# Recurrent stage of a hybrid decoder step: z and y with features on partitions, the gate behind the transposition, sums of squares by products with ones

## The chip, the cores and the metric

One core of a Trainium2 chip. The metric is the device time of one execution in microseconds, median of the runs. All tensors of this stage are float32; a float32 matrix product is two instructions on TensorE for each 128-row block of weights.

## The reference

One step of a decoder layer, for a prompt of 1024 rows and 8 sample rows. The change touches the Mamba-2 branch. In it 2048 inner features are 4 groups of 512 (8 heads of 64), and the scan goes over 8 chunks of 128 rows. Per group and chunk:

```
y = y_diag + y_off + d_skip * x                # the chunked scan
y = y * silu(z)                                # z = h @ w_in[:, 0:2048]
yg = y.reshape(B, L, 4, 512)
yg = yg * rsqrt(mean(yg * yg, axis=-1) + 1e-6)
y = yg * norm_g                                # then projected by the next stage
```

The sample rows take one step of the same recurrence with their own states, read from memory and written back.

## The kernel before

The function ssm holds the stage. Each engine runs a program of its own, in the order written; semaphores tie them. PSUM has eight banks of 128 x 512.

For each of 4 groups there is a z part, then a scan.

**z part.** TensorE makes z with rows on partitions: 16 units (z_unit), each 8 products of 256 columns into bank 1 or 2, which ScalarE's Silu takes to SBUF (L1740). After every 8 units z_samples makes the sample rows' z with features on partitions, 32 instructions of 8 columns (L1602, two z_samples a group). In between stand the turn of the last chunk before, raw_rows (L1611, L1617), and two spreads (L1628) of the sample rows' B and C, after which VectorE updates half of the sample states (L1851 to L1868). The states' buffer is exchanged by DMA between the halves; in groups 1 and 2 the sync queue does this behind a weight load that waits until half of z is done. The part ends with the samples' sum of squares (L1656).

**Scan.** For chunk c TensorE's order is: front(c + 1), the x/B/C units of the next group but the last one (unit, L1514, 8 products of 344 columns each; 3, 3, 2, 2, 2, 2, 2, 2 units in the chunks), back(c), turn(c - 1), and the last unit. Group 3 has no units. front is: B turned and C·B (L1532, L1533) into bank 0; x turned (L1538) into bank 3; segment sums (L1544). back is: y_diag (L1557), y_off (L1564), state product (L1572). turn transposes y of a chunk into bank 0 (L1581).

VectorE: in front, mask and B copy from bank 0 (L1892, L1893), xdt (L1898), mask product (L1903); in back, y additions (L1914 to L1922), gate by z (L1925), state scaled and added (L1935, L1937), then the mean (L1940); in scale, reciprocal and product by it (L1946, L1947); then, in some chunks, the convolution of a finished x/B/C block (L1803 to L1807), which waits until ScalarE has kept its last unit.

ScalarE: copy of x (L1701) and Exp (L1705) of the next chunk, Silu of a convolved block, copies of units (keep, L1694), out: four copies scaled by norm_g from bank 0 (L1725), then norm: Square with its sum by row (L1713) and Sqrt of one column (L1716).

GpSimd: xw, xd (L1485, L1487), segments of the next chunk (L1453), and the store of turned y (L1446).

## Time and profile before

| what | us |
|---|---|
| median of 3 runs | 3235.45 (3233.89 to 3241.91) |
| profiled execution, its own time | 3245.16 |
| its span | 3243.4 |
| recurrent stage, first product to last store issued | 1105.8 to 1972.1 |
| TensorE busy in the span | 2934.5 (90%) |
| VectorE busy | 1595.4 (49%) |
| ScalarE busy | 729.8 (23%) |
| GpSimd busy | 715.6 (22%) |

The stage is 27% of the span. Times in the rows below are in us from the span's start, means of groups in ns. A bracket behind a row is the engine's idle time ahead of it and what ended that. In the names PE is TensorE's products, PEld its weight loads, DVE VectorE, ACT ScalarE, POOL GpSimd. A row of a timeline merges equal instructions that follow each other; its length goes to the end of the last, which still runs when the next instruction starts.

### The profile page before, as it was taken

Reading aid. Unit: us, or ns where it says so; the run is one execution under the profiler, and the core shown is the slowest. Engines: PE = TensorE matmul, PEld = TensorE weight load, DVE = VectorE, ACT = ScalarE, POOL = GpSimd, SP = SyncE. Lnnn points to the kernel's source line nnn. Section 1 sums busy time; section 2 is a strip of 40 time slices with the busy share of each in tenths; the row PEclk is TensorE's granted clock in tenths of the full one; section 3 lists DMA queues with packets and bytes.
Section 4 is the critical chain, followed back from the end, with each engine's and each line's share of the span. In section 5 each row is a group of like instructions: output and inputs, shape, how many; then the busy total and the mean of one; then the engine's idle time right before and its main releaser. Section 6 shows DMA issues by size and latency. Waiting matters only on the chain. (4 is left out here: it accounts for less than half of the span.)

```text
span 3243.4 us, 39578 instructions
## 1 busy us (share of the span) xinstructions
PE 2934.5 (90%) x15831; PEld 2380.4 (73%) x15831; DVE 1595.4 (49%) x2860; ACT 729.8 (23%) x1511; POOL 715.6 (22%) x430
## 2 busy tenths in 40 slices
PE   6999999989986679999999974999879999999997
PEld 3888566657874556676775854999869898898986
DVE  1313499625541456536546464254563544445355
ACT  4121211126761114424324242000030000000001
POOL 0000520023200122222122232323232232232320
PEclk7999999989995779999999977999989999999999
DMA  6110245410012230121120105233211111111111
GB/s 194 37 66 20 66 137 162 129 49 2 2 39 73 94 86 23 47 78 39 48 75 29 40 26 186 78 112 98 88 31 60 39 39 53 39 46 46 40 40 53
DMA packets 220308, 211.59 MB, mean 65 GB/s; under 512 B 15257, under 2 KB 201489, under 8 KB 219938
## 3 DMA queue, kind: packets, MB, share of 16 engines
q1 hardware_dynamic: 195580, 162.36, 16.5%
q10 hardware_dynamic: 20944, 34.86, 3.1%
q0 software_dynamic: 3600, 11.82, 0.9%
q8 instruction: 127, 2.08, 0.3%
q14 instruction: 57, 0.47, 0.0%
HBM read 165.32 MB, written 43.83 MB: 64 GB/s over the span
## 5 line engine op out<-in xcount | busy, mean ns | idle before, releaser
L2052 PE MATMUL ps<-h_lo,w_hi 128*128 128x344 f32 x1504 | 483.0, 321 | 40.3 <-DVE h_lo L2160 33.5
L2054 PE MATMUL ps<-h_hi,w_lo 128*128 128x344 f32 x1504 | 481.5, 320 | 0.0
L2053 PE MATMUL ps<-h_hi,w_hi 128*128 128x344 f32 x1504 | 481.5, 320 | 0.0
L2052 PEld LDWEIGHTS ps<-h_lo,w_hi 128*128 128x128 f32 x1504 | 284.2, 189 | 42.0 <-issue 35.4
L2053 PEld LDWEIGHTS ps<-h_hi,w_hi 128*128 128x128 f32 x1504 | 283.9, 189 | 0.2
L2054 PEld LDWEIGHTS ps<-h_hi,w_lo 128*128 128x128 f32 x1504 | 284.0, 189 | 0.0
L2034 POOL CAST w_hi<-w_raw 128x2048 fp32r<-128x2048 f32 (+1 forms) x50 | 97.3, 1945 | 838.1 <-PE ps L2054 803.4
L1514 PE MATMUL ps<-hT,ring 128*128 128x344 f32 x864 | 266.7, 465 | 0.0
L1593 PE MATMUL ps<-ring,hT 128*128 128x256 f32 x1024 | 236.3, 393 | 7.8 <-PEq L1164 6.7
L453 PE MATMUL ps<-ring,hT 128*128 128x256 f32 (+3 forms) x1152 | 238.1, 369 | 1.0 <-PEq L214 1.0
L1514 PEld LDWEIGHTS ps<-hT,ring 128*128 128x128 f32 x864 | 168.2, 197 | 92.6 <-issue 19.1
L2036 POOL TENSOR_TENSOR w_lo<-w_raw,w_hi 128x2048 fp32r<-128x2048 f32 (+1 forms) x50 | 233.7, 4673 | 4.0
L1593 PEld LDWEIGHTS ps<-ring,hT 128*128 128x128 f32 x1024 | 201.4, 198 | 42.0 <-issue 11.0
L604 PE MATMUL ps<-hT,ring 128*128 128x344 f32 x768 | 229.6, 459 | 0.0
L453 PEld LDWEIGHTS ps<-ring,hT 128*128 128x128 f32 (+1 forms) x1152 | 197.4, 182 | 39.1 <-issue 3.8
L604 PEld LDWEIGHTS ps<-hT,ring 128*128 128x128 f32 x768 | 145.7, 192 | 82.5 <-issue 5.4
L2440 ACT ACTIVATE f_silu<-ps 128x344 f32<-128x344 f32 x66 | 30.3, 459 | 734.6 <-PE ps L2054 734.6
L2473 DVE TENSOR_TENSOR f_prod<-ps,f_silu 128x344 f32<-128x344 f32 x66 | 34.1, 516 | 326.0 <-ACT f_silu L2440 326.0
L667 DVE TENSOR_SCALAR_CACHE_REDUCE reached<-score,threshold_bits 128x384 uint8<-128x384 f32 (+5 forms) x192 | 171.5, 943 | 38.8 <-POOL score L560 36.6
L2052 PE MATMUL ps<-w_lo,a_hi 128*128 128x512 f32 (+1 forms) x396 | 158.1, 399 | 21.4 <-DVE f_scaled L2486 21.4
L874 DVE CUSTOM_DVE_ANT_0 prob<-ps,sel_bias 128x128 f32<-128x128 f32 (+7 forms) x128 | 96.8, 756 | 153.0 <-PE ps L805 151.6
L2053 PE MATMUL ps<-w_hi,a_hi 128*128 128x512 f32 (+1 forms) x396 | 156.4, 395 | 0.0
(393 smaller groups left out, 5025.5 us busy)
## 6 DMA issues: line engine op xcount, KB each, us to landing
ring<-in_w_ada SPq DMA_DIRECT2D x24, 1024.0 KB, 7.5
ring<-in_w_in SPq DMA_DIRECT2D x23, 1024.0 KB, 5.2
w_raw<-in_w_ffn_in SPq DMA_DIRECT2D x44, 512.0 KB, 5.2
ring<-in_w_in SPq DMA_DIRECT2D x24, 512.0 KB, 8.3
w_raw<-in_w_ffn_out SPq DMA_DIRECT2D x10, 1024.0 KB, 5.0
s_sig<-sig ACTq DMA_DIRECT2D x16, 516.0 KB, 6.9
x<-s_sig ACTq DMA_DIRECT2D x16, 516.0 KB, 3.4
stt<-in_state_ssm SPq DMA_DIRECT2D x32, 256.0 KB, 3.9
```

Source lines behind the costliest of these rows:

```text
L453: mm = nc.tensor.matmul(ps[0:r, (9 * s + t) % 4, 0:width], hT[:, k, P * t:P * t + r], w[:, k, 0:width], start=(k == 0), stop=(k == KB - 1))
L604: mm = nc.tensor.matmul(ps[:, j % 4, 0:CW], w[:, k, 0:P], hT[:, k, CW * c:CW * c + CW], start=(k == 0), stop=(k == KB - 1))
L667: a = v.tensor_scalar(reached[:, at:at + P * (i + 1)], score_of(i), thr_f[:, i:i + 1], None, ALU.is_ge, ALU.add, accum_out=count[:, i:i + 1])
L874: nc.vector.tensor_tensor_reduce(out=prob[:, n % 2, 0:L], in0=ps[:, 2 * (n % 2):2 * (n % 2) + 2, :].rearrange("p a n -> p (a n)")[:, chunk ...
L1514: a = mm(ps[:, 6 + u % 2, 0:CW], w[:, k, P * (f % 2):P * (f % 2) + P], hT[:, k, CW * c:CW * c + CW], start=(k == 0), stop=(k == KB - 1))
L1593: a = mm(ps[:, 1 + u % 2, 0:256], hT[:, k, P * t:P * t + P], w[:, k, :], start=(k == 0), stop=(k == KB - 1))
L2034: self.nc.gpsimd.tensor_copy(hi, raw).then_inc(self.hi_done, 1)
L2036: self.nc.gpsimd.tensor_tensor(lo, raw, hi.bitcast(F32), ALU.subtract).then_inc(self.split, 1)
L2052: nc.tensor.matmul(out, ah, bl, start=(i == 0), stop=False)
L2053: nc.tensor.matmul(out, ah, bh, start=False, stop=False)
L2054: mm = nc.tensor.matmul(out, al, bh, start=False, stop=(i == len(terms) - 1))
L2473: v.tensor_tensor(prod[:, i % 2, :], ps[:, 2 * (i % 3) + 1, 0:CW], silu[:, i % 2, :], ALU.mult).then_inc(act_done, 1)
```

## The change

z is made with features on partitions: 12 units a group (4 feature blocks x 3 column parts of 344, which contain the sample rows), so z_samples goes. y is no longer gated and normalized before it is turned: turn takes it as soon as it is summed. VectorE then multiplies the turned y in PSUM by z (gate). ScalarE squares it; GpSimd adds the halves of the squares (fold); TensorE sums them over partitions with two products by a tile of ones into bank 0 (sum_squares), which also spreads the sum over all partitions. ScalarE takes the root from PSUM with scale 1/512 and bias 1e-6 (root). VectorE takes its reciprocal, 128 x 128, and multiplies (divide); ScalarE scales by norm_g in place (out). In front the product for bank 0 moves behind the segment sums and waits for a root instead of an output. The order of each engine's steps changes with it; in chunk c: gate and square of c - 1, division and output of c - 2. In the z part raw rows and spreads move to units 8 and 10 in group 0, and to 1, 3 and 9 in the others. In SyncE's queue the weight loads behind z wait for 6 and 12 units instead of the two sample products. Cut to its core:

```diff
+    def fold(g, c):
+        n = TT * g + c
+        pool.wait_ge(ysquared, n + 1)
+        v.tensor_tensor(ysq2[:, 0:2 * P], ysq2[:, 0:2 * P], ysq2[:, 2 * P:4 * P], ALU.add).then_inc(yfolded, 1)
...
             if c + 1 < TT:
                 segments(g, c + 1)
             if c >= 2:
-                store(g, c - 2)
+                fold(g, c - 2)
+            if c >= 3:
+                store(g, c - 3)
+        fold(g, TT - 2)
+        store(g, TT - 3)
+        fold(g, TT - 1)
         store(g, TT - 2)
         store(g, TT - 1)
...
-        if n:
-            pe.wait_ge(cb_done, 2 * n)
         if g and c == 0:
-            pe.wait_ge(yT_done, n)
             pe.wait_ge(s_done, n)
         if c >= 2:
-            pe.wait_ge(yT_done, n - 2)
             pe.wait_ge(s_done, n - 1)
-        tr(ps[:, 0, P:2 * P], post[:, 4, cols], K.ident[:])
-        mm(ps[:, 0, 0:P], post[:, 4, cols], post[:, 5, cols], start=True, stop=True).then_inc(bcb_ps, 1)
...
+        if n:
+            pe.wait_ge(cb_done, 2 * n)
+        if g and c == 0:
+            pe.wait_ge(yroot2, n)
+        if c >= 3:
+            pe.wait_ge(yroot2, n - 2)
+        tr(ps[:, 0, P:2 * P], post[:, 4, cols], K.ident[:])
+        mm(ps[:, 0, 0:P], post[:, 4, cols], post[:, 5, cols], start=True, stop=True).then_inc(bcb_ps, 1)
...
     def turn(g, c):
         n = TT * g + c
-        pe.wait_ge(ynormed, n + 1)
+        pe.wait_ge(*((y_ready, n - g) if c else (yd_done, 2 * (n + 1))))
         pe.wait_ge(cb_done, 2 * min(n + 3, TT * (g + 1)))
-        if c == TT - 1:
-            pe.wait_ge(yT_done, n)
+        if c >= TT - 2:
+            pe.wait_ge(yroot2, n)
         for j in range(4):
             t = tr(ps[:, 0, P * j:P * j + P], y[:, c % 2, P * j:P * j + P], K.ident[:])
         t.then_inc(yT_ps, 1)

+    def sum_squares(g, c):
+        pe.wait_ge(yfolded, TT * g + c + 1)
+        for j in range(2):
+            a = mm(ps[:, 0, 0:P], K.ones[:], ysq2[:, P * j:P * j + P], start=(j == 0), stop=(j == 1))
+        a.then_inc(ysum_ps, 1)
...
-        i, t, w = u // TT, u % TT, slab_of(K, slab(g, 3 + u // TT))
-        if t == 0:
-            pe.wait_ge(*ring_landed(K, slab(g, 3 + i)))
...
-            pe.wait_ge(z_done, 2 * TT * g + u - 1)
...
-            a = mm(ps[:, 1 + u % 2, 0:256], hT[:, k, P * t:P * t + P], w[:, k, :], start=(k == 0), stop=(k == KB - 1))
+            a = mm(ps[:, 1 + u % 2, 0:CW], w[:, k, P * (f % 2):P * (f % 2) + P],
+                   hT[:, k, CW * c:CW * c + CW], start=(k == 0), stop=(k == KB - 1))
         a.then_inc(z_ps, 1)
-
-    def z_samples(g, i):
-        w = slab_of(K, slab(g, 3 + i))
-        if g:
...
-        for fb in range(2):
-            for k in range(KB):
-                a = mm(ps[:, 4, DEC * (2 * i + fb):DEC * (2 * i + fb) + DEC], w[:, k, P * fb:P * fb + P],
-                       hT[:, k, SEQ:NT], start=(k == 0), stop=(k == KB - 1))
-        a.then_inc(zs_ps, 1)
...
-        raw_at, spread_at = (1, 4) if g else (10, 13)
-        for u in range(2 * TT):
+        raw_at, spread_at = (1, 3) if g else (8, 10)
+        for u in range(ZU):
             z_unit(g, u)
-            if u == 0 and g:
+            if g and u == 0:
                 turn(g - 1, TT - 1)
                 final_state(g - 1)
+            if g and u == 1:
+                sum_squares(g - 1, TT - 1)
             if u == raw_at:
                 raw_rows(g)
             if u == spread_at:
                 spread(g, 0)
-            if g and u == 12:
+            if g and u == 9:
                 spread(g, 1)
-            if u % TT == TT - 1:
-                z_samples(g, u // TT)
         if g == 0:
             spread(g, 1)
...
+            if c:
+                sum_squares(g, c - 1)
     turn(GROUPS - 1, TT - 1)
+    sum_squares(GROUPS - 1, TT - 1)
...
-    def norm(g, c):
+    act.wait_ge(eps_set, 1)
...
+    def square(g, c):
         n = TT * g + c
         act.wait_ge(ygated, n + 1)
         if n:
-            act.wait_ge(ysquared, n)
-        a.activation(ysq2[:], y[:, c % 2, :], ACT.Square, accum_out=stat[:, 0, c % 2:c % 2 + 1])\
-            .then_inc(ysquared, 1)
-        act.wait_ge(ymean, n + 1)
-        a.activation(stat[:, 2, c % 2:c % 2 + 1], stat[:, 1, c % 2:c % 2 + 1], ACT.Sqrt).then_inc(yroot2, 1)
+            act.wait_ge(ysum_ps, n)
+        a.activation(ysq2[:], yT[:, c % 2].rearrange("p k n -> p (k n)"), ACT.Square).then_inc(ysquared, 1)
+
+    def root(g, c):
+        n = TT * g + c
+        act.wait_ge(ysum_ps, n + 1)
+        if n:
+            act.wait_ge(ynormed, n)
+        a.activation(spreads[:, 0, :], ps[:, 0, 0:P], ACT.Sqrt, bias=eps[:, 0:1], scale=1.0 / GW).then_inc(yroot2, 1)

...
-        act.wait_ge(yT_ps, n + 1)
-        if n >= 2:
-            act.wait_ge(yT_out[c % 2], 16 * (n // 2))
+        act.wait_ge(ynormed, n + 1)
         for j in range(4):
             k = 136 + 4 * g + j
-            o = a.activation(yT[:, c % 2, j, :], ps[:, 0, P * j:P * j + P], ACT.Copy, scale=K.vecs[:, k:k + 1])
+            o = a.activation(yT[:, c % 2, j, :], yT[:, c % 2, j, :], ACT.Copy, scale=K.vecs[:, k:k + 1])
...
-        for u in range(2 * TT):
-            i, t = u // TT, u % TT
-            act.wait_ge(z_ps, 2 * TT * g + u + 1)
+        for u in range(ZU):
+            f, c = u // TC, u % TC
             if g and u == 0:
-                act.wait_ge(ygated, TT * g)
-            a.activation(z[:, t, 256 * i:256 * i + 256], ps[:, 1 + u % 2, 0:256], ACT.Silu).then_inc(z_done, 1)
+                out(g - 1, TT - 2)
+                square(g - 1, TT - 1)
+            act.wait_ge(z_ps, ZU * g + u + 1)
+            a.activation(zT[:, f, CW * c:CW * c + CW], ps[:, 1 + u % 2, 0:CW], ACT.Silu).then_inc(z_done, 1)
             if u == 0 and g:
+                keep_final(g - 1)
+            if u == 1 and g:
+                root(g - 1, TT - 1)
                 out(g - 1, TT - 1)
-                keep_final(g - 1)
...
+            if c >= 2:
+                out(g, c - 2)
             if c:
-                out(g, c - 1)
+                square(g, c - 1)
             for j in units[-1:]:
                 keep(g + 1, j)
-            norm(g, c)
+            if c:
+                root(g, c - 1)
...
+    out(GROUPS - 1, TT - 2)
+    square(GROUPS - 1, TT - 1)
+    root(GROUPS - 1, TT - 1)
...
-                link(v.tensor_tensor(yc, yc, t, ALU.add), ystep, ny)
-            else:
-                dve.wait_ge(yd_done, 2 * (n + 1))
-            v.tensor_tensor(yc, yc, z[:, c, :], ALU.mult).then_inc(ygated, 1)
+                v.tensor_tensor(yc, yc, t, ALU.add).then_inc(y_ready, 1)
...
-            i = c % 2
-            dve.wait_ge(ysquared, n + 1)
-            v.tensor_scalar(stat[:, 1, i:i + 1], stat[:, 0, i:i + 1], 1.0 / GW, EPS, ALU.mult, ALU.add).then_inc(ymean, 1)
...
-        def scale(c):
+
+        def gate(c):
             n = TT * g + c
-            i = c % 2
+            dve.wait_ge(yT_ps, n + 1)
+            if n >= 2:
+                dve.wait_ge(yT_out[c % 2], 16 * (n // 2))
+            v.tensor_tensor(yT[:, c % 2], ps[:, 0, :].rearrange("p (k n) -> p k n", k=4), zT[:, :, P * c:P * c + P],
+                            ALU.mult).then_inc(ygated, 1)
+
+        def divide(c):
+            n = TT * g + c
             dve.wait_ge(yroot2, n + 1)
-            link(v.reciprocal(stat[:, 3, i:i + 1], stat[:, 2, i:i + 1]), ystep, ny)
-            v.tensor_scalar(y[:, i, :], y[:, i, :], stat[:, 3, i:i + 1], None, ALU.mult).then_inc(ynormed, 1)
+            v.reciprocal(spreads[:, 0, :], spreads[:, 0, :]).then_inc(yinv, 1)
+            dve.wait_ge(yinv, n + 1)
+            v.tensor_tensor(yT[:, c % 2], yT[:, c % 2], spreads[:, 0, :].unsqueeze(1).to_broadcast([P, 4, P]),
+                            ALU.mult).then_inc(ynormed, 1)
...
         front(0)
         for c in range(TT):
             if c + 1 < TT:
                 front(c + 1)
             back(c)
-            scale(c)
+            if c >= 2:
+                divide(c - 2)
+            if c:
+                gate(c - 1)
             if g + 1 < GROUPS:
                 for f in blocks_at[c]:
                     convolve(g + 1, f)
+        divide(TT - 2)
+        gate(TT - 1)
+        divide(TT - 1)

```

## Rows read from the trace of the kernel before

**Rows 1.** Stretches: length, busy PE, PEld, DVE, ACT, POOL, granted clock, DMA.
```profile
1105.81:1165.02 59.21, 59.21 (x269) 51.62 (x269) 30.17 (x42) 12.99 (x23) 6.14 (x7) 0.90 0.27 87
1247.75:1352.69 104.94, 97.02 (x392) 63.94 (x391) 68.81 (x94) 47.59 (x83) 23.73 (x20) 0.95 0.11 36
1473.35:1579.83 106.48, 98.55 (x393) 64.73 (x392) 68.83 (x94) 47.57 (x83) 23.75 (x20) 0.94 0.10 35
1698.72:1802.35 103.63, 95.70 (x392) 63.30 (x391) 68.82 (x94) 47.57 (x83) 23.75 (x20) 0.97 0.10 36
1352.69:1428.00 75.31, 73.65 (x357) 63.24 (x356) 29.22 (x50) 14.84 (x34) 15.50 (x15) 0.94 0.25 72
1579.83:1653.48 73.65, 71.99 (x358) 61.81 (x356) 29.22 (x50) 14.84 (x34) 15.50 (x15) 0.96 0.25 74
1802.35:1876.31 73.96, 72.30 (x357) 62.15 (x356) 29.22 (x50) 14.84 (x34) 15.50 (x15) 0.95 0.18 51
1902.94:1950.64 47.70, 35.38 (x140) 23.22 (x141) 30.54 (x52) 24.98 (x45) 18.78 (x16) 0.79 0.05 21
```

**Rows 2.** TensorE's timeline in group 3's z part (start, length, line, operation).
```profile
1824.21 10.52 PE L1593 MATMUL ps<-ring,hT 128*128 128x256 f32 x48
1834.57 3.63 PE L1602 MATMUL ps<-hT,ring 128*128 128x8 f32 x32
1838.06 19.20 PE L1593 MATMUL ps<-ring,hT 128*128 128x256 f32 x80
1857.09 1.88 PE L1628 MATMUL ps<-bc_diag,ones 128*128 128x512 f32 x4
...
1873.91 1.88 PE L1656 MATMUL ps<-ysq,ones 128*128 128x8 f32 x8 [0.81 <-DVE ysq L1874]
```

**Rows 3.** VectorE's timeline, end of the sample work in that part.
```profile
1869.61 0.19 DVE L1871 TENSOR_TENSOR ysum<-ysum,xdt_s 128x32 f32<-128x32 f32 x1
```

**Rows 4.** TensorE's timeline in the scan of group 2.
```profile
1718.97 0.27 PE L1532 MATMUL ps<-ident,post 128*128 128x128 f32 x1
...
1727.82 1.08 PE L1564 MATMUL ps<-state,post 128*128 128x512 f32 x2
...
1730.03 4.79 PE L1514 MATMUL ps<-hT,ring 128*128 128x344 f32 x16
1734.66 0.27 PE L1532 MATMUL ps<-ident,post 128*128 128x128 f32 x1
...
1747.22 1.10 PE L1572 MATMUL ps<-xw,btok 128*128 128x512 f32 x2 [2.64 <-DVE xdt L1898]
...
1753.22 0.27 PE L1532 MATMUL ps<-ident,post 128*128 128x128 f32 x1
...
1765.79 1.31 PE L1572 MATMUL ps<-xw,btok 128*128 128x512 f32 x2 [2.64 <-DVE xdt L1898]
...
1773.47 0.27 PE L1532 MATMUL ps<-ident,post 128*128 128x128 f32 x1
```

**Rows 5.** VectorE's timeline there: the state addition of the first chunk.
```profile
1731.71 0.69 DVE L1937 TENSOR_TENSOR state<-state,ps 128x512 f32<-128x512 f32 x1
```

**Rows 6.** VectorE's groups of instructions (xcount | busy us, mean ns): reciprocals.
```profile
L1946 DVE RECIPROCAL ssm_stat<-ssm_stat 128x1 f32<-128x1 f32 x32 | 5.2, 164 | 39.8 <-ACT ssm_stat L1716 39.8
...
L1279 DVE RECIPROCAL dt_t<-dt_t 128x264 f32<-128x264 f32 x1 | 1.8, 1802 | 0.0
```

**Rows 7.** GpSimd's groups of instructions: an addition of two SBUF tiles.
```profile
L559 POOL TENSOR_TENSOR score<-score,score_term 128x384 f32<-128x384 f32 x3 | 3.0, 992 | 0.2
```

**Rows 8.** ScalarE's timeline in the scan of group 2.
```profile
1681.68 1.28 ACT L1705 ACT_TABLE_LOAD   x1
1682.98 1.02 ACT L1705 ACTIVATE m<-ps 128x1024 f32<-128x1024 f32 x1
...
1719.52 0.63 ACT L1713 ACTIVATE ssm_ysq<-ssm_y 128x512 f32<-128x512 f32 x1
...
1730.23 1.14 ACT L1725 ACTIVATE ssm_yT<-ps,vecs 128x128 f32<-128x128 f32 x4 [3.50 <-PE ps L1581]
```

More of the change, by code:

```diff
@@ L1320, in ssm @@
         posts = sb("post", [P, 2, FBS, SEQ])
-        z = sb("z", [P, TT, GW])
+        zT = sb("zT", [P, 4, NT])
         tail = sb("tail", [P, FBS, 11])
@@ L1326, in ssm @@
         cx, ct = sb("cx", [P, FBS, DEC]), sb("ct", [P, FBS, DEC])
-        zs, xdt_s = sb("zs", [P, 4, DEC]), sb("xdt_s", [P, 4, DEC])
+        xdt_s = sb("xdt_s", [P, 4, DEC])
         bc_diag = sb("bc_diag", [P, 2, 4, P])
@@ L1340, in ssm @@
         yT = sb("ssm_yT", [P, 2, 4, P])
-        stat = sb("ssm_stat", [P, 4, 2])
+        spreads = sb("ssm_rms", [P, 1, P])
+        eps = sb("ssm_eps", [P, 1])
         fin = sb("fin", [P, 4, P])
@@ L1359, in ssm @@
         yo_done, s_scaled, s_done, yd_done = K.sem("yoff_done"), K.sem("state_decayed"), K.sem("state_done"), K.sem("ydiag_done")
-        ystep, ygated, ysquared, ymean, yroot2, ynormed = (K.sem(n) for n in (
-            "y_step", "y_gated", "y_squared", "y_mean", "y_root", "y_normed"))
+        y_ready, ygated, ysquared, yfolded, ysum_ps, yroot2, yinv, ynormed = (K.sem(n) for n in (
+            "y_ready", "y_gated", "y_squared", "y_squares_folded", "y_squares_summed", "y_root", "y_inverse", "y_normed"))
         yT_ps, yT_done, yT_out = K.sem("ssm_yT_in_psum"), K.sem("ssm_yT_done"), [K.store_sem(f"ssm_yT_stored{i}") for i in range(2)]
@@ L1364, in ssm @@
         old_out = K.store_sem("old_conv_rows_stored")
+        eps_set = K.sem("eps_set")
         block = ctx.enter_context(nc.Block())
+        ZU = 4 * TC
         here = [3, 3, 2, 2, 2, 2, 2, 2]
@@ L1442, in _ @@
             v = nc.gpsimd
+            v.memset(eps[:], EPS).then_inc(eps_set, 1)
             v.memset(pre[:, :, 0:CONV - 1], 0.0).then_inc(conv_step, 1)
@@ L1783, in _ @@
             v = nc.vector
-            nconv, nss, ny = [0], [0], [0]
+            nconv, nss = [0], [0]
             def link(ins, sem, count):
```

23 lines of the change are left out of this document (12 added, 11 removed).

## The prediction

> **What bounds the kernel now.** I read the page's totals first, to see which engine is nearly full: TensorE is, so its idle time is what can be won, and what is added to it is paid. Then the busy time by stretch, cut at the edges of the recurrent stage's parts [rows 1]. The stage runs from about 1105.8 to 1972 us. In each of the four groups a z part (sums for z, and the sample rows' states beside them) is followed by a scan of eight chunks. In the scans of groups 0 to 2 the x/B/C sums of the next group fill TensorE (97.02 of 104.94 us busy). In the scan of group 3 nothing fills it: 35.4 of 47.7 us busy in four chunks, granted clock 0.79 [rows 1]. There a loop of waits sets the time, 47.70 / 4 = 11.93 us a chunk. The timelines of the engines then show what sets each part.
>
> In a z part TensorE has 16 units of 3.45 us (three of them from 1824.21 to 1834.57) and twice 32 products of 8 columns for the sample rows, 3.49 us each time (1834.57 to 1838.06) [rows 2]. The 5 units behind the first of these took 19.03 us (1838.06 to 1857.09) instead of 17.25. VectorE's sample work ends 12.7 us after the second spread (1857.09 to 1869.80) [rows 2, 3]: there is slack before 1873.91 now, but not much.
>
> In the scan of group 2 a chunk without other waits takes 15.69 us (1718.97 to 1734.66); where a convolution ran before, the state product waits 2.64 us for xdt. Behind one such wait TensorE needed 7.68 us for state product, turn and unit (1765.79 to 1773.47), behind another 6.00 (1747.22 to 1753.22): its clock had fallen to the lower level in the first and not in the second [rows 4].
>
> **The change part by part.**
>
> *z in 12 units of 344 columns.* The removed 256-column units and the new ones have the same work: 16 x 3.45 = 55.2 us against 12 x 4.63 = 55.6 us, 4.63 us being what a unit of this shape takes now (1730.03 to 1734.66) [rows 4]. The sample products go: 2 x 3.49 us. Groups 1 to 3, counted from the end of the last x/B/C unit: up to the second spread there are now 13 units, one set of sample products, 1.8 us of slower clock (19.03 against 17.25), and 4.6 us of other things (1857.09 - 1802.35 = 54.7). After it: 10 units (46.3), the same 4.6, two new sums of squares at 0.44 each: 51.8. Then VectorE's sample work, which no longer hides behind 3 units and samples (13.9 us) but only behind 2 units (9.3 us): 12.7 us and two small operations, 0.5 with their gaps, until the sum may start, 13.2. With the 2.40 us up to the scan's first product (1873.91 to 1876.31) that makes 67.4 us against 75.31, 73.65 and 73.96 [rows 1, 2, 3]: -7.9, -6.3, -6.6. The second half of the states reaches VectorE barely in time: its exchange now starts after 6 units, and I estimate that it is complete about 1 us before it is needed.
> Group 0: the raw rows come after 9 units, not 11, and the first spread after 11 units, not 14. The 59.21 us up to it are 14 units (48.3), one set of sample products (3.5) and 7.4 of raw rows and slow clock [rows 1]. Of the 7.4 I let half go with the sample products, behind which the clock was slow, as in rows 2, and keep 3.9 for raw rows and the start: 11 x 4.63 + 3.9 = 54.8. What follows waits for the states' transfer, which that spread sets off. So only 4.4 us of the larger saving counts.
> z parts: **-25 us**.
>
> *The y chain.* VectorE loses the wait for Square and for Sqrt. It loses 0.69 (gate), 0.49, 0.16 and 0.15 us of work, and gets a gate from PSUM (0.69), a reciprocal of 128x128 and a product of 128x512 (0.69). No row shows that reciprocal. With one column it took 164 ns, with 264 columns 1802 ns: (1802 - 164) / 263 = 6.2 ns a column, so 0.95 us [rows 6]. The bounds are 0.16 and 1.80; the slope decides for 0.95. The fold on GpSimd (two inputs in SBUF, 256 columns) lies below the 0.992 us of 384 columns and above two thirds of it, 0.66: I take 0.72 [rows 7]. The root on 128 columns from PSUM I take as 0.37, above a quarter of the 1.14 us that four such operations took together, which overlap [rows 8]; it lies on the chain only at the end. The sum of squares is four passes of 128 columns, 0.44 us (as four transposes), 0.85 at the low clock.
>
> All of this hangs in one chain in program order, and TensorE, also in order, stands at its end. Sum of squares c-1 comes ahead of everything of the next chunk. It needs: VectorE's state addition of chunk c, division c-2, gate c-1; ScalarE's output scaling c-2, then Square c-1; GpSimd's fold. In groups 0 to 2 one x/B/C unit is to cover that.
> Let Y be the start of the y_off product (1727.82). VectorE started the state addition at Y + 3.89 (1731.71); without the gate ahead, 0.72 less, Y + 3.17. Reciprocal at Y + 3.78, product at 4.77, done 5.46. Output scaling holds ScalarE 1.0 us before Square may start: 6.49, done 7.12 (0.63) [rows 4, 5, 8]. Fold done 7.91, sum of squares at Y + 7.95. TensorE by itself is there at Y + 6.84 (1734.66). So it stands 1.1 us in each chunk. From the sum's start to Y it has 8.85 (1718.97 to 1727.82) + 0.44 = 9.29. Period: 9.29 + 7.95 = 17.24 us.
> The convolution is no longer late: it starts as soon as the last unit is kept, and no longer behind Square, mean, Sqrt, reciprocal and scaling, so the three waits of 2.64 us and the slow units behind them go. Chunks 2 to 6 of a group take 5 x 17.24 = 86.2, chunk 7 without a front 0.44 + 4.63 + 1.73 + 7.95 = 14.75: 101.0 against 104.94, 106.48 and 103.63 [rows 1, 4]. That is -12 us in three groups; chunk 0 and 1 stay (chunk 1 has two units ahead and no division yet). For slower clock after the new stops I put 15 x 0.4 = 6 us back, between 0 and 1.7 each (below). Scans 0 to 2: **-6 us**.
>
> *Group 3's scan.* Now the loop closes with the state addition: TensorE's next front starts when it is done. After, it closes with the sum of squares. Behind the state addition's start that is 4.78 us (7.95 - 3.17) where it was 0.72, so +4.06; the sum itself at the low clock +0.85; the gate out of the chain -0.72. The product for B/C moved behind the segment sums takes 0.6 out of the path to Exp, but mask, B copy and xdt now come after it and delay the mask product by 0.7; that product no longer meets GpSimd's segments and takes about 0.7 less. Sum: +3.6, 15.5 us a chunk. It is paid four times between front 3 and front 7 (+14). The start gains 1. The last two chunks pay more, since nothing is left to overlap: front 7's chunk +4, chunk 7 +5, then behind the last state addition. There, where scaling, turn and store took 5 us, stand division, output scaling, Square, fold, sum, root, division, gate, Square, fold, sum, root, division, output scaling and two stores, some 15.5 us at the prices above: +10; less 3 us that turn and division overlap: +16 for the end. Group 3's scan: **+29 us**.
>
> What only moves is hidden: the table load for the root lies beside fold and sum (1.28 against 0.72 + 0.6) [rows 8], and two more in the z part beside 4.6 us units. Stores start later, but land before their buffer is written.
>
> Sum: -25 - 6 + 29 = -2 us. The profiled execution took 3245.16 us, its span 3243.40; the median of the runs is 3235.45, 0.3% less. The difference carries over: 3235.45 - 2 = 3233.
>
> A page's price against this, in sentences of its own. Every switch of ScalarE's table took 1.28 us here, and Exp started with no gap behind it (1681.68, 1682.98) [rows 8]. The Trainium skill (ScalarE: Activation LUTs, "What ACT_TABLE_LOAD costs") adds 1.38 us of drain to each switch, 2.66 in all. By that the root would end 1.3 us later and delay the copy of x behind it; group 3's loop would be about 0.5 us longer, and my -2 would be +2. The trace decides for 1.28.
>
> **The rivals.**
>
> *The clock falls at each new stop (slower).* Of the nine stops of 2.64 us in groups 0 to 2, seven were followed by the lower level, and then 1.7 us were lost (7.68 against 6.00) [rows 4]. If the 1.1 us stops do this as well, 15 x 1.7 = 26 instead of 6: +18, 3253. It decides (over +0.3%) from about 1.2 us a stop. Against it: the stop is shorter, and dense units stand right ahead. Beside this: the Trainium skill (TensorE: Matmul & The Clock Gate, "HAM oscillation") tells of a kernel whose array was throttled again in every iteration by a wait. The trace shows this after 2.64 us, and not after every one.
>
> *The chain is shorter than I price it (faster).* If reciprocal or fold cost what their narrow rows show, or the output scaling from SBUF goes faster, 0.75 us or more leaves the chain. Then TensorE hardly stands: 15 x 0.75 = 11, the clock's 6, and 7 x 0.75 = 5 in group 3 go: -22, 3211; half of it 3222.
>
> *The states' transfer becomes the bound of the z parts.* In groups 1 and 2 I estimate 1 us of slack; if it comes 3 us late and group 0 gains nothing, z gives -15: +8, 3243. That the change gives no saving here at all is excluded by the 28 us of sample products gone, which nothing covers in groups 1 to 3.
>
> **How the numbers follow.** Forecast 0.45, its own range 3222 to 3246; clock 0.20; shorter chain 0.25; states 0.10. Within 0.3% (9.7 us) is what a measurement of this kernel can't tell from no change. Of the forecast 0.06 lies on the faster side of that and 0.04 on the slower; of the clock 0.17 are slower; of the shorter chain 0.20 faster; of the states 0.04 slower. Faster 0.26, same 0.49, slower 0.25. The range takes in most of the clock's case and half of the shorter chain's: 3214 to 3254.
>
> **What would show it.** Right: sum-of-squares products with about 1.1 us of TensorE idle ahead, released by GpSimd's fold, in chunks 2 to 6; no wait for xdt; group 3's chunks near 15.5 us; reciprocals of 0.95 us; z parts of 67 us with 2 us idle ahead of the samples' sum. Wrong: a reciprocal far off 0.95, a scan of group 3 that keeps its present length, or a mean clock under 0.94 in the scans of groups 0 to 2.

## The result, and the profile after

| | forecast | measured |
|---|---|---|
| median, changed kernel | 3233 (3214 to 3254) | 3246.05 us (3241.13 to 3249.25, 15 runs) |
| median, kernel before, beside it | 3235.45 | 3238.44 us (3233.89 to 3247.67, 15 runs) |
| ratio | 0.999 | 1.0018, 95% interval 1.0009 to 1.0026 |

The changed kernel is slower: its median lies 7.6 us (0.23%) higher, and the ratio of all its runs to those of the kernel before is 0.18% over 1. That is less than the 0.3% which the prediction called "same", and 3246 lies in its range, but the interval excludes both "no change" and the small gain that was forecast.

The busy time of the changed kernel by stretch (start, end and length; then busy us of PE, PEld, DVE, ACT, POOL with instructions in brackets; granted clock, DMA share, GB/s): chunks 2 to 7 of groups 0, 1, 2, three z parts, and the scan of group 3.

```profile
1242.93:1346.84 103.91, 95.80 (x417) 63.60 (x415) 71.49 (x90) 49.91 (x79) 31.61 (x26) 1.00 0.10 34
1456.89:1560.80 103.91, 95.80 (x417) 63.60 (x415) 71.48 (x90) 49.89 (x79) 31.59 (x26) 1.00 0.10 34
1672.68:1776.60 103.92, 95.80 (x417) 63.62 (x415) 71.50 (x90) 49.90 (x79) 31.60 (x26) 1.00 0.10 34
1346.84:1412.62 65.78, 63.28 (x236) 41.63 (x237) 31.87 (x50) 17.63 (x34) 17.89 (x18) 1.00 0.31 92
1560.80:1626.86 66.06, 63.55 (x237) 41.90 (x237) 31.87 (x50) 17.64 (x34) 17.89 (x18) 0.99 0.31 93
1776.60:1842.38 65.78, 63.28 (x237) 41.63 (x237) 31.85 (x50) 17.64 (x34) 17.90 (x18) 1.00 0.22 65
1842.38:1970.70 128.32, 75.96 (x314) 50.78 (x314) 64.52 (x96) 46.18 (x78) 42.68 (x40) 0.76 0.04 15
```

Against [rows 1]: the three stretches of six chunks, which took 103.6 to 106.5 us at a clock of 0.94 to 0.97, now take 103.9 each at 1.00. The z parts fell from 75.31, 73.65 and 73.96 to about 65.9. The scan of group 3 went from 95.8 us (1876.31 to 1972.09) to 128.32, and its clock is 0.76. In this pair of traces the whole stage took 866.28 us before and 865.98 after (1104.72 to 1970.70).

The timeline of chunk 2 to 3 of group 2, which answers to [rows 4, 5]:

```profile
1703.28 0.94 DVE L1974 RECIPROCAL ssm_rms<-ssm_rms 128x128 f32<-128x128 f32 x1
...
1704.98 1.28 ACT L1745 ACTIVATE ssm_yT<-ssm_yT,vecs 128x128 f32<-128x128 f32 x4 [6.57 <-DVE ssm_yT L1976]
...
1705.54 0.81 DVE L1831 TENSOR_SCALAR post<-pre,vecs 128x1024 f32<-128x1024 f32 x1
1706.17 0.61 ACT L1731 ACTIVATE ssm_ysq<-ssm_yT 128x512 f32<-128x512 f32 x1
...
1706.86 1.39 POOL L1464 TENSOR_TENSOR ssm_ysq<-ssm_ysq 128x256 f32<-128x256 f32 x1 [11.01 <-ACT ssm_ysq L1731]
...
1708.30 0.71 PE L1603 MATMUL ps<-ssm_ysq,ones 128*128 128x128 f32 x4 [1.79 <-POOL ssm_ysq L1464]
...
1725.05 0.72 POOL L1464 TENSOR_TENSOR ssm_ysq<-ssm_ysq 128x256 f32<-128x256 f32 x1 [10.64 <-ACT ssm_ysq L1731]
1725.32 1.28 ACT L1738 ACT_TABLE_LOAD   x1
...
1725.82 0.71 PE L1603 MATMUL ps<-ssm_ysq,ones 128*128 128x128 f32 x4 [1.13 <-POOL ssm_ysq L1464]
...
1726.61 0.37 ACT L1738 ACTIVATE ssm_rms<-ps,ssm_eps 128x128 f32<-128x128 f32 x1
```

The order is the one foreseen: reciprocal, output scaling (four in 1.28 us), Square, fold, and TensorE waiting for it: 1.13 us at 1725.82. Where a convolution starts on VectorE (1705.54) the fold takes 1.39 us instead of 0.72 and the stop is 1.79. The table load ends at 1726.60 and the root starts at 1726.61. Two chunks of group 3, the sums and what they wait for:

```profile
1867.32 1.22 PE L1603 MATMUL ps<-ssm_ysq,ones 128*128 128x128 f32 x4 [5.05 <-POOL ssm_ysq L1464]
...
1881.34 0.61 ACT L1731 ACTIVATE ssm_ysq<-ssm_yT 128x512 f32<-128x512 f32 x1
...
1882.03 0.72 POOL L1464 TENSOR_TENSOR ssm_ysq<-ssm_ysq 128x256 f32<-128x256 f32 x1 [7.82 <-ACT ssm_ysq L1731]
...
1882.80 1.22 PE L1603 MATMUL ps<-ssm_ysq,ones 128*128 128x128 f32 x4 [6.30 <-POOL ssm_ysq L1464]
```

15.48 us from sum to sum, 6.3 of them TensorE's idle time behind the fold.

### The profile page after: what moved, and what is told of

It is laid out like the page before. It is cut to its first block and busy times, and to the rows that moved or that the text cites. A ratio compares the mean times of both kernels' runs of the same rounds, so it can differ in the third digit from the quotient of the medians.

```text
span 3239.2 us, 38780 instructions
## 1 busy us (share of the span) xinstructions
PE 2897.3 (89%) x15447; PEld 2298.8 (71%) x15447; DVE 1610.9 (50%) x2828; ACT 732.0 (23%) x1457; POOL 754.2 (23%) x463
## 5 line engine op out<-in xcount | busy, mean ns | idle before, releaser
L1528 PE MATMUL ps<-hT,ring 128*128 128x344 f32 x864 | 257.8, 452 | 0.0
L1616 PE MATMUL ps<-hT,ring 128*128 128x344 f32 x768 | 227.9, 457 | 6.8 <-PEq L1164 6.8
L604 PE MATMUL ps<-hT,ring 128*128 128x344 f32 x768 | 227.2, 455 | 0.0
L1528 PEld LDWEIGHTS ps<-hT,ring 128*128 128x128 f32 x864 | 160.7, 190 | 77.6 <-issue 1.4
L1616 PEld LDWEIGHTS ps<-hT,ring 128*128 128x128 f32 x768 | 146.6, 192 | 84.9 <-issue 13.1
L604 PEld LDWEIGHTS ps<-hT,ring 128*128 128x128 f32 x768 | 144.3, 190 | 80.9 <-ACT sig L639 5.4
L2090 PE MATMUL ps<-w_hi,a_lo 128*128 128x512 f32 (+1 forms) x396 | 155.7, 393 | 0.0
```

The source lines that it names most:

```text
L604: mm = nc.tensor.matmul(ps[:, j % 4, 0:CW], w[:, k, 0:P], hT[:, k, CW * c:CW * c + CW], start=(k == 0), stop=(k == KB - 1))
L1528: a = mm(ps[:, 6 + u % 2, 0:CW], w[:, k, P * (f % 2):P * (f % 2) + P], hT[:, k, CW * c:CW * c + CW], start=(k == 0), stop=(k == KB - 1))
L1616: a = mm(ps[:, 1 + u % 2, 0:CW], w[:, k, P * (f % 2):P * (f % 2) + P], hT[:, k, CW * c:CW * c + CW], start=(k == 0), stop=(k == KB - 1))
L2090: mm = nc.tensor.matmul(out, al, bh, start=False, stop=(i == len(terms) - 1))
```

## The experiments

Medians are compared with the changed kernel's 3246.05 us, ratios are to runs of the kernel before on the same chip. The two can disagree by some us: on the four chips of these experiments the kernel before itself had medians of 3241.31 to 3244.68, not 3238.44. "Stage" is taken from a kernel's own trace, from the first z product to the end of the last store of y; it leaves out the final state's store, which makes it 0.7 us shorter than above. In the changed kernel it is 865.1 to 867.6 us, by four traces; it holds nothing of the rest of the program, so it is the safer comparison.

### The z part from both sides

`before_few_samples`: the kernel before with one of the eight products of each sum for the sample rows' z; the sums over the other seven blocks of rows are left out.

```diff
-                    for k in range(KB):
+                    for k in range(1):
                         a = mm(ps[:, 4, DEC * (2 * i + fb):DEC * (2 * i + fb) + DEC], w[:, k, P * fb:P * fb + P],
```

> The kernel before with 2 of the 16 products in each of the eight sets of the sample rows' z (the sum over the other seven blocks of rows is left out). Everything else and all waits stay. Theory of my forecast: a set takes 3.5 us and slows the clock behind it by about 2 us, so 8 sets give about 24 us, and in groups 1 to 3 the samples' own chain behind the second spread gives 3 us of that back once per group: 3.1 + 2 saved ahead of it, 0 to 3 behind. Expected 17 to 22 us faster. Rival (the clock behind the sets has nothing to do with them, and the chain of the sample states already sets the z parts): under 10 us faster.

Measured: 3208.74 us (3205.91 to 3210.65), ratio 0.9895 [0.988, 0.991], stage 826.5 us: 34 us less than the kernel before by the ratio, well over the expectation. Its trace of group 3's z part (TensorE):

```profile
1804.87 0.51 PE L1602 MATMUL ps<-hT,ring 128*128 128x8 f32 x4
1805.23 17.51 PE L1593 MATMUL ps<-ring,hT 128*128 128x256 f32 x80
1822.58 1.88 PE L1628 MATMUL ps<-bc_diag,ones 128*128 128x512 f32 x4
```

A set went from 3.63 to 0.51 us, and the five units behind it from 19.20 [rows 2] to 17.51. That makes some 8 us a group. The steps between the samples' sums of squares became 216.5, 214.2 and 211.7 us, from 225.8, 225.5 and 222.8, so 9 to 11 each. Not all of this is the z part's: from the last x/B/C unit to the samples' sum the three z parts lost 9.1, 7.3 and 8.2 us, but the scans of groups 1 and 2, whose code is the same, lost 4.0 and 2.9 us as well. Of the nine waits for xdt five are followed by slow units in this trace, against seven in that of the kernel before. So about 7 us of the saving lie in the scans. Whether taking out the products brought that about, or this execution showed another of the kernel's own patterns, one trace can't tell; as a price of the sample products alone 34 us is too much.

`after_idle_samples`: the changed kernel with the old sample products put back: 32 of 8 columns each time, into columns of bank 5 that nobody reads.

```diff
+                    if u % 6 == 5:
+                        idle_samples(g, u // 6)
                     z_unit(g, u)
```

> The changed kernel with the kernel before's sample products put back, 32 products of 8 columns ahead of z unit 5 and 32 ahead of unit 11 of each group, into columns of bank 5 that nobody reads (their result is not used). It undoes the saving of the z part alone. Theory: in groups 1 to 3 each set costs its 3.49 us and the slower clock behind it 1.8, less the 2.1 us that TensorE waits for the samples' sum anyway: 4 to 6 us a group, and little in group 0, which waits for the states' transfer: +13 to +20, 3259 to 3266. Rival: what the kernel before lost by these products is what taking out seven eighths of them there gave, 34 us, since each set also costs the clock for long behind it: +30 or more, 3276.

Measured: 3278.40 us (3277.14 to 3282.57), ratio 1.0112 [1.0096, 1.0129], stage 895.7 us: +32 us by the medians and +30.5 by the stage, the rival's size. TensorE in group 3's z part:

```profile
1827.71 3.63 PE L1624 MATMUL ps<-hT,ring 128*128 128x8 f32 x32
1831.20 23.38 PE L1616 MATMUL ps<-hT,ring 128*128 128x344 f32 x80
...
1856.13 4.79 PE L1616 MATMUL ps<-hT,ring 128*128 128x344 f32 x16
1860.76 4.23 PE L1624 MATMUL ps<-hT,ring 128*128 128x8 f32 x32
1864.84 7.64 PE L1616 MATMUL ps<-hT,ring 128*128 128x344 f32 x16
1873.55 1.06 PE L1679 MATMUL ps<-ysq,ones 128*128 128x8 f32 x8 [1.07 <-DVE ysq L1910]
```

The first set costs its 3.49 us alone. The second costs 4.08 (1860.76 to 1864.84), and the unit behind it 7.64 instead of 4.79; only 1.0 of the 2.1 us ahead of the samples' sum hides it. That is 9.4 us a group, and it is measured at 8 to 9 (steps of 225.3, 222.1 and 224.0 us against 216.4, 214.0 and 215.8), and group 0, where I expected little, pays 4.8. So the size was the rival's, without its reason: one unit behind the second set is slow, not many. The z part alone is worth about 30 us, and the scans give it all back.

### The links of the chain

`after_narrow_recip`: the reciprocal works on 1 of its 128 columns; the other 127 stay roots.

```diff
-                    v.reciprocal(spreads[:, 0, :], spreads[:, 0, :]).then_inc(yinv, 1)
+                    v.reciprocal(spreads[:, 0, 0:1], spreads[:, 0, 0:1]).then_inc(yinv, 1)
```

> The changed kernel with VectorE's reciprocal on 1 column in place of 128 (the other 127 columns are multiplied by the root itself: the norm is left out for them). 0.95 us becomes 0.16. Theory (the chain state addition, division, gate, output scaling, Square, fold, sum of squares sets each chunk's end): 0.78 us less in each of the 18 stops of groups 0 to 2, and in 6 to 7 chunks and twice at the end of group 3: 14 + 7 = 21 us faster, and stops of 0.3 to 1.0 us where 1.13 and 1.8 stood. Rival (TensorE's own work sets the chunks and the stops only move): under 5 us faster.

Measured: 3224.87 us (3221.14 to 3233.36), ratio 0.9948 [0.9931, 0.9965], stage 844.4 us: -21 us, as expected. The stop of 1.13 us becomes 0.34 (`after_narrow_recip`, TensorE, group 2):

```profile
1712.37 0.71 PE L1603 MATMUL ps<-ssm_ysq,ones 128*128 128x128 f32 x4 [0.34 <-POOL ssm_ysq L1464]
```

The reciprocal fell from 946 to 156 ns: 0.79 us, all of which left the stop. VectorE is 69% busy in those chunks, yet this operation costs its full length, because the chain passes through it.

`after_no_fold`: TensorE sums four blocks of squares instead of two folded ones.

```diff
-                v.tensor_tensor(ysq2[:, 0:2 * P], ysq2[:, 0:2 * P], ysq2[:, 2 * P:4 * P], ALU.add)
...
-                pe.wait_ge(yfolded, TT * g + c + 1)
-                for j in range(2):
+                pe.wait_ge(ysquared, TT * g + c + 1)
+                for j in range(4):
```

> The changed kernel without GpSimd's fold: TensorE sums the four blocks of squares by four products instead of two of folded ones. Theory: the fold stands in the exposed chain, with 0.72 us, and with 1.39 us where a convolution starts beside it; without it the stop ahead of the sum is 0.38 us everywhere, and two more products cost 0.44 us (0.85 at the low clock). Net 0.3 us in 15 chunks of groups 0 to 2 and 1.0 us in 6, 0.3 us in seven chunks of group 3: 10 to 14 us below the changed kernel, 3232 to 3236, which is below the kernel before. Rival: the convolution is what is late, and the fold beside it only looks long; then the stops of 1.79 us shrink as the others do, by 0.75, and the whole is -6 or less, 3240.

Measured: 3236.67 us (3234.36 to 3237.89), ratio 0.9976 [0.9965, 0.9986], stage 855.7 us: -9 us, just short of the 10 to 14 expected, and below the kernel before. TensorE in group 2, at the sum beside which a convolution starts:

```profile
1703.28 1.16 PE L1599 MATMUL ps<-ssm_ysq,ones 128*128 128x128 f32 x8 [0.33 <-ACT ssm_ysq L1727]
```

All 18 stops of groups 0 to 2 are 0.32 or 0.33 us, those of 1.13 and of 1.79 alike. So the longer fold, and not a late convolution, made the longer stop. In group 3 there is little: stops of 5.0 to 6.2 us in the middle, and four products at the low clock.

### The chain's place

`after_sum_late`: the chain's work is unchanged, but TensorE takes the sum of chunk c - 2, and ScalarE the root of it, behind the next front, in chunks 2 to 7. The last sum but one stays where it was. The sums go to bank 4 (bank 6 in group 3); front waits for the gate instead of the root, and y_off for the root.

```diff
                         front(g, c + 1)
+                    if c > 1:
+                        sum_squares(g, c - 2)
...
-                    if c:
+                    if c and (c == TT - 1):
                         sum_squares(g, c - 1)
```

> The changed kernel with TensorE's sum of squares of chunk c - 1, and ScalarE's root of it, moved one place later, behind the front of chunk c + 2, in chunks 0 to 5 of each group. The sum goes to bank 4 (bank 6 in group 3), so that bank 0 is free after the gate. Theory: TensorE's 1.1 to 1.8 us stop in each chunk of groups 0 to 2 and the 5 to 6.5 us stop in each chunk of group 3 are the price of the chain's place in the program, not of its work. Then the stops of chunks 1 to 6 go (about 4 x 1.13 + 2 x 1.8 = 8 us a group, 24 in three), and group 3's period falls from 15.2 us to about 12 us for five chunks (16 to 20): 40 to 44 us below the changed kernel, near 3203, which would beat both kernels. Rival: the chain only finds another door. The root with its table load now holds ScalarE before the x/B/C copies, and y_off waits for the root: then stops of about 1 us come back at y_off or at the units, and only 10 to 20 us are won, 3226 to 3236.

Measured: 3218.88 us (3216.79 to 3220.11), ratio 0.9927 [0.9914, 0.9941], stage 839.4 us: -27 us, between theory and rival. In groups 0 to 2 the stops ahead of the sums of chunks 1 to 4 are gone; those of chunks 5 and 6 keep theirs, 1.79 and 1.13 us, since chunk 7 has no front to stand behind and the last but one was not moved (two chunks of group 2; TensorE):

```profile
1712.09 1.88 PE L1552 MATMUL ps<-seg,gt 128*128 128x512 f32 x4
...
1714.14 0.61 PE L1611 MATMUL ps<-ssm_ysq,ones 128*128 128x128 f32 x4
1714.59 4.79 PE L1528 MATMUL ps<-hT,ring 128*128 128x344 f32 x16
...
1722.73 1.10 PE L1590 MATMUL ps<-xw,btok 128*128 128x512 f32 x2 [0.71 <-DVE xdt L1938]
```

A wait of 0.71 us for xdt came back in one chunk of each group. In group 3 the period is 13.2 us, not 12: y_off waits 1.33 us for the root, and VectorE's mask product takes 3.70 us beside GpSimd's products, where it took 1.69 in the changed kernel (at 1873.60, beside the last 0.6 us of one). Of these two it is the mask product that counts: the next two experiments have no such wait at y_off in group 3, and their period is 13.2 us as well, with the mask product at 3.69 to 3.71 us (all engines of `after_sum_late`, group 3):

```profile
1865.99 1.04 POOL L1494 TENSOR_TENSOR xw<-xt,s_ddt 128x512 f32<-128x512 f32 x1
...
1866.99 1.04 POOL L1496 TENSOR_TENSOR xd<-xt,heads_row 128x512 f32<-128x512 f32 x1
...
1867.27 3.70 DVE L1943 TENSOR_TENSOR m<-m,cbm 128x1024 f32<-128x1024 f32 x1 [1.59 <-ACT m L1731]
1867.99 1.89 POOL L1457 TENSOR_TENSOR seg<-le,s_dta 128x1024 f32<-128x1024 f32 x1
1868.55 0.37 ACT L1749 ACTIVATE ssm_rms<-ps,ssm_eps 128x128 f32<-128x128 f32 x1
...
1869.06 1.10 PE L1582 MATMUL ps<-state,post 128*128 128x512 f32 x2 [1.33 <-ACT ssm_rms L1749]
```

`after_sum_late_g3`: the same in group 3 alone.

```diff
+                    if c > 1 and g == GROUPS - 1:
+                        sum_squares(g, c - 2)
```

> The same move in group 3 alone; groups 0 to 2 as in the changed kernel. Theory: the +32 us of group 3's scan come from the loop that closes with the fold; with the sum behind the next front five chunks go from about 15.2 to 12 us, 16 to 20 us below the changed kernel (3226 to 3230), which by itself turns the sign against the kernel before. Rival: VectorE's work of a chunk, 8.7 us with the reciprocal, and the turned order set the period as well; then it stays above 14 us and at most 6 us are won (3240).

Measured: 3230.07 us (3228.34 to 3230.89), ratio 0.9959 [0.9945, 0.9972], stage 848.7 us: -16 us. Half of group 3's loss was the sum's place; taking that alone back makes the changed kernel faster than the kernel before. Its period is 13.2 us though y_off waits for nothing (TensorE, group 3):

```profile
1879.29 0.71 PE L1607 MATMUL ps<-ssm_ysq,ones 128*128 128x128 f32 x4 [1.41 <-POOL ssm_ysq L1464]
...
1892.48 0.71 PE L1607 MATMUL ps<-ssm_ysq,ones 128*128 128x128 f32 x4
...
1894.77 1.08 PE L1580 MATMUL ps<-state,post 128*128 128x512 f32 x2
```

`after_sum_later`: the late sum in the last two chunks too. In groups 0 to 2 the sum of chunk 5 stands behind the x/B/C unit of chunk 7. In group 3 all sums go to banks 6 and 7, y_off waits for no root, and at the end the gate of chunk 6 comes ahead of division 5 and its Square ahead of scaling 5.

```diff
                     back(g, c)
+                    if c == TT - 1 and g == GROUPS - 1:
+                        sum_squares(g, c - 2)
...
                     if g and u == 0:
+                        sum_squares(g - 1, TT - 2)
                         turn(g - 1, TT - 1)
```

> The version with the late sum, carried to the last two chunks of each group: the sum of chunk 5 behind the x/B/C unit of chunk 7 (in group 3 behind back of chunk 7), the sum of chunk 6 behind the first z unit of the next group (in group 3 behind the last turn); in group 3 all sums go to banks 6 and 7, so that y_off does not wait for a root, and at its end the gate of chunk 6 and its Square come ahead of the division and scaling of chunk 5. Theory: the stops that are left in that version, 1.79 and 1.13 us in the last two sums of each group, go as well (3 x 2.9 = 9 us), in group 3 the 1.3 us ahead of y_off (up to 6 us) and some 6 us of the two 5.3 us stops at its end: 12 to 20 us below 3218.9, 3199 to 3207. Rival: where nothing fills TensorE, VectorE's mask product, which takes 3.7 us there beside GpSimd's products, sets the period of group 3, and the end is a chain of fixed length: then only the 9 us of groups 0 to 2 come, 3210.

Measured: 3211.78 us (3210.98 to 3215.14), ratio 0.9896 [0.9881, 0.9911], stage 834.4 us: 7 us less than `after_sum_late` by the medians, 5 by the stage, but from the other end than the rival said. From the samples' sum to the last store group 3 takes 106.9 us instead of 117.1. Its period stayed at 13.2 us, in which the rival was right; what fell was the end, which the rival had called a chain of fixed length. Groups 0 to 2 lost 3 us twice (steps of 214.3, 209.8 and 213.4 us against 211.2, 209.8 and 210.7), for a new stop took the place of the old ones (TensorE, start of group 1's z part):

```profile
1347.22 0.61 PE L1613 MATMUL ps<-ssm_ysq,ones 128*128 128x128 f32 x4
1347.66 0.60 PE L1601 MATMUL ps<-ident,ssm_y 128*128 128x128 f32 x4
1351.46 0.63 PE L1660 MATMUL ps<-ident,state 128*128 128x128 f32 x4 [3.19 <-ACT ssm_rms L1757]
1351.92 6.49 PE L1626 MATMUL ps<-hT,ring 128*128 128x344 f32 x16
```

The final state needs bank 4, which holds the sum until its root is taken, and the unit behind the 3.19 us stop is slow.

`after_sum_best`: the final state behind the second z unit.

```diff
                         turn(g - 1, TT - 1)
-                        final_state(g - 1)
                     if g and u == 1:
+                        final_state(g - 1)
                         sum_squares(g - 1, TT - 1)
```

> The version with the late sum in all chunks, with the final state turned behind the second z unit of the next group instead of behind the first, so that its bank's wait for the root of chunk 6 is covered. Theory: the 3.2 us stop ahead of the final state, which ate what the last two sums had given in groups 0 to 2, goes, together with the slow unit behind it: 3 x 3 = 9 us or a little more below 3211.8, 3200 to 3204. Rival: the first two z units then wait for ScalarE, which stands at the root of chunk 6, and the stop only moves to the third unit: 3210.

Measured: 3212.32 us (3206.95 to 3213.10), ratio 0.9904 [0.9888, 0.9921], stage 832.7 us: no change beyond the spread. The rival was right: the same time is lost one step on, ahead of the last sum.

```profile
1350.48 0.60 PE L1660 MATMUL ps<-ident,state 128*128 128x128 f32 x4
1353.48 0.71 PE L1613 MATMUL ps<-ssm_ysq,ones 128*128 128x128 f32 x4 [2.40 <-POOL ssm_ysq L1464]
```

The version without the fold and the four with the late sum beat both kernels; the last two are 1% under the kernel before.

### Several traces of the two kernels

The kernel before was traced seven more times (`before_same`, `before_again`, `before_third`, `before_fourth`, `before_look5` to `before_look7`), the changed kernel three more (`after_same`, `after_third`, `after_fourth`). Their expectations were:

> The kernel before, unchanged, profiled once more. In the first pair of profiles the recurrent stage took 866.3 us before and 866.0 after, yet the medians differ by 7.6 us. Theory A (the sum was made from one execution in which TensorE's clock fell more often than it usually does): here the stage is shorter than 866.3, most likely by 5 to 12 us, all of it in stretches where the granted clock was below 1 the first time (scans of groups 0 to 2, units behind the sample products). Theory B (the two stages are equal, and the 7.6 us arise outside, after or before the stage): the stage takes 866 us within 2 again, and what lies outside it differs.

> The changed kernel, unchanged, profiled once more. The profiled execution was the fastest of 15 (3241.1, median 3246.05). Theory A: this one is nearer the median, and the difference is slow clock: in group 3's scan, or behind the stops of 1.1 to 1.8 us ahead of the sums of squares, which had the full clock the first time. Theory B: the stage takes 866 us within 2 again and the difference to the first profile lies outside it.

> The kernel before once more, for its trace. Theory A: its executions differ by how often the clock falls at the waits for xdt in the recurrent stage; an execution near 3235 would show a stage some 8 us shorter than the 866 us of the two traces so far (3245 and 3247). Theory B: the stage is 866 us in all of them, and what differs lies ahead of it or behind it.

> The kernel before for its trace, a fourth time. The three so far took 3244.5 to 3247.0 us by their own time, all with a stage of 866 us and seven clock falls of nine waits for xdt. Theory A: an execution near 3235 has a shorter stage (fewer falls, 858 us or less). Theory B: the stage is 866 us there too, and it is what lies before and after the stage that is shorter.

> As the one before it: the kernel before once more, theory A a stage of 858 us or less in an execution near 3235, theory B 866 us in every execution.

> The kernel before for its trace. All five traces so far are of executions of 3244.5 to 3249.0 us with a mean granted clock of 0.933 to 0.935, while the timed executions go from 3234 to 3251 us and the fast ones list 0.937 to 0.939. Theory A: the 10 us by which the fast ones are shorter lie in the recurrent stage, as clock falls that do not happen: a trace of an execution under 3240 us shows a stage of 858 us or less and fewer falls behind the waits for xdt. Theory B: they lie outside the stage, where both kernels have the same code: the stage is 866 us in it, and the rest 2367 to 2372 us instead of 2377 to 2382.

> As the look before it. Theory A: in an execution under 3240 us the stage is 858 us or less. Theory B: it is 866 us, and the rest is shorter.

> As the look before it. Theory A: in an execution under 3240 us the stage is 858 us or less. Theory B: it is 866 us, and the rest is shorter.

> The changed kernel for its trace. The kernel before has two stage lengths in eight traces: 865.6 to 866.4 us five times, 861.0 to 861.1 three times, those three in executions of 3239.9 to 3242.5 us; the clock's pattern in the scan of group 3 and in group 2 differs. The changed kernel showed 865.3 and 866.6 us in two traces. Theory A: it has no short pattern to lose or win, since its stops in groups 0 to 2 don't let the clock fall and its group 3 runs at the low level throughout: the stage is 865 to 867 us again. Theory B: it has one too, and the two traces missed it: 861 us or less.

> As the look before it: theory A a stage of 865 to 867 us, theory B 861 us or less in one of the two.

Measured (own time; the stage; the rest of the span, where both kernels have the same code):

| trace | own time | stage | rest |
|---|---|---|---|
| before | 3245.16 | 865.5 | 2377.9 |
| before_same | 3246.98 | 865.8 | 2379.4 |
| before_again | 3244.50 | 866.3 | 2376.4 |
| before_third | 3248.64 | 866.3 | 2380.5 |
| before_fourth | 3248.97 | 866.3 | 2380.9 |
| before_look5 | 3242.45 | 861.0 | 2379.6 |
| before_look6 | 3239.93 | 861.1 | 2377.0 |
| before_look7 | 3240.31 | 861.0 | 2377.5 |
| after | 3241.13 | 865.2 | 2374.0 |
| after_same | 3248.10 | 866.6 | 2379.4 |
| after_third | 3243.59 | 865.1 | 2376.6 |
| after_fourth | 3248.15 | 867.6 | 2378.5 |

The kernel before has two stage lengths, 866 and 861 us; the changed kernel has 865 to 868 only, in four traces. The 861 us lie between what the theories said (858 or 866), so theory A holds in kind and for half the size. The busy time of the middle of group 3's scan shows where most of it is, first of `before_same`, then of `before_look6`:

```profile
1899.00:1947.00 48.00, 35.60 (x144) 23.51 (x144) 30.85 (x53) 24.96 (x44) 19.15 (x17) 0.79 0.05 22
```

```profile
1895.00:1943.00 48.00, 33.72 (x162) 22.69 (x161) 33.27 (x53) 25.98 (x45) 21.34 (x18) 0.89 0.05 22
```

The clock is 0.89 instead of 0.79, and TensorE gets through 162 instead of 144 instructions in the same 48 us. From the samples' sum of group 3 to the last store that is 94.2 us against 97.4 to 97.5. The rest is one clock fall: behind the second wait for xdt of group 1 the state product, turn and unit take 8.8 to 8.9 us in the five traces of 866 and 6.0 in the three of 861 (TensorE, `before_same`, then `before_look6`):

```profile
1523.79 2.04 PE L1572 MATMUL ps<-xw,btok 128*128 128x512 f32 x2 [2.64 <-DVE xdt L1898]
...
1532.63 0.27 PE L1532 MATMUL ps<-ident,post 128*128 128x128 f32 x1
```

```profile
1523.51 1.10 PE L1572 MATMUL ps<-xw,btok 128*128 128x512 f32 x2 [2.64 <-DVE xdt L1898]
...
1529.51 0.27 PE L1532 MATMUL ps<-ident,post 128*128 128x128 f32 x1
```

The traces of 861 us give 1.4 us of this back in the last z part, which takes 72.93 us in `before_look6` and 71.56 in `before_same`. Of the nine waits for xdt seven are followed by slow units in the former, six in the latter.

## Why the prediction was wrong

**The step that failed** is the last line of the sum: "The difference carries over: 3235.45 - 2 = 3233." A gain of 2 us was forecast and the medians show a loss of 7.6. The sum over the stage was nearly right for the pair of traces it was made for: -2 forecast, -0.3 measured (866.28 to 865.98). Part of that is luck, since its three terms were off by -4.2, +2.4 and +3.5 us. But the traced execution lay 9.7 us over the median, and this was subtracted from the changed kernel as well. About 5 us of it were the kernel before's own: its traced execution had the stage of 866 us, while others of the same kernel have 861. The changed kernel has no such shorter stage in four traces. Against 861 us the stage's change is +4 to +7 us, against 866 it is -1 to +2.

How much of the 7.6 us this explains depends on how often the kernel before runs with the short stage. Its traces with 866 us took 3244.5 us or more, those with 861 took 3239.9 to 3242.5; 12 of the 15 timed executions took 3242.62 or less, so the short stage, or a still shorter time, was probably the usual one. That is an inference from the times: 8 of the 15 were shorter than any execution that was traced. The remaining 2 to 3 us are not settled. Of 40 timed executions of the kernel before that list a mean granted clock, those under 3238.4 us list 0.936 to 0.939 and those over 3246.0 list 0.932 to 0.934. That the shortest have a still shorter stage was only argued; the rest of the program, which has taken 2374.0 to 2380.9 us in the traces of the two kernels, may be what is short in them. Another part of the 13 us between 3233 and 3246 is the reference itself: the median of three runs that the forecast started from was 3235.45, that of fifteen 3238.44.

Point by point:

- **z parts, -25.** Measured -3.9, -9.5, -7.6 and -8.2, together -29.2. Mechanism right, the size 4 us too small. TensorE waits 2.09 us for the samples' sum (forecast 2); in the three z parts of groups 1 to 3 the clock is 0.99 to 1.00, where I had kept some of the slow clock. With the products put back the loss is 30 to 32 us.
- **Scans 0 to 2, -6.** Measured -3.6, from two errors that nearly cancel. The period is 17.53 us (forecast 17.24), since the scaling from SBUF holds ScalarE for 1.28 us, not 1.0; where a convolution starts it is 18.2, since the fold takes 1.39, not 0.72. Six chunks take 103.9 us where 101.0 were forecast: 3 x 2.9 = +8.7. In turn the 6 us put back for slower clock were not needed: behind the stops of 1.13 to 1.80 us the clock stayed at 1.00. The waits for xdt and the slow units behind them went, as forecast.
- **Group 3, +29.** Measured +32.5. Chunks of 13.8 to 16.1 us (forecast 15.5), waiting for the fold for 4.9 to 6.5 us. `after_sum_late_g3` shows the mechanism for half of it: without touching the chain's work, 16 us come back.
- **Prices of the new operations.** Reciprocal 0.946 us (forecast 0.95), fold 0.72 (0.72) without a convolution, root 0.367 (0.37), gate 0.68 (0.69). The estimates from slopes of narrower and wider rows held; the two prices missed were those that I took as independent of place (scaling from SBUF) or of neighbours (fold).
- **Table loads.** The root starts 0.01 us behind its load. The Trainium skill (ScalarE: Activation LUTs, "What ACT_TABLE_LOAD costs") would have 1.38 us of drain there; this trace shows none.
- **The rivals.** The clock did not fall at the new stops of groups 0 to 2: in all four traces of the changed kernel the six chunks take 103.9 us in each of these groups, at a granted clock of 1.00. So this rival falls too, though the time came out on its side. The Trainium skill (TensorE: Matmul & The Clock Gate, "HAM oscillation") describes stops in a loop that throttle the array; here the lower clock followed on six or seven of nine stops of 2.64 us, and on none of those of 1.1 to 1.8 us. The shorter chain did not come either, but `after_narrow_recip` shows that its price was right: it said 22 us for 0.75 us off the chain, and 0.79 us give 21.

## What to carry to other kernels

A time forecast from one traced execution should say which of the kernel's own patterns that execution shows: trace the kernel before several times, and ask whether the kernel before has a faster pattern that the change removes, before "the difference carries over". An in-order engine pays for a chain at the place where it waits for it, and only for what nothing covers there; moving the wait behind independent work gave back 27 us, while shortening the chain by one reciprocal gave 21. After each such move look at which bank or which engine the consumer now holds: twice here the stop only came back one step later.

## What was not expected of the hardware

- GpSimd's addition of 128x256 took 0.72 us alone and 1.39 us while VectorE ran a convolution; VectorE's mask product of 128x1024 took 1.69 us nearly alone and 3.70 beside GpSimd's products. Each then took about twice its time.
- Sets of products with 8 columns cost more than their length: behind the second of two such sets a unit took 7.64 instead of 4.79 us (`after_idle_samples`).
- With equal code the granted clock in the middle of group 3's scan was 0.79 in one execution and 0.89 in another, and the first took 3 us more for the scan.
